# Two denoiser layers on one core: where the branch products of a weight piece stand in TensorE's order

## Chip, core and metric

The kernel runs on one core of a Trainium2 chip. The metric is the time of one execution on the device in microseconds. Three runs of the kernel before gave 1427.73, 1430.44 and 1431.5; the median is 1430.44.

## What is computed

Two layers run over 640 tokens: 128 of a context and 512 latent ones. Each layer normalises and modulates the tokens, projects them, runs four token mixers (A convolution, B grouped attention, C retention, D differential attention), projects each mixer's output to 1024 columns, weighs it with a sigmoid gate made from the same input, adds the four and projects the sum. What the change touches is this (cut from the reference):

```python
gates = jax.nn.sigmoid(h @ p["w_mgate"])
merged = None
for i, y in enumerate(branches):
    term = gates[..., i * D_MODEL:(i + 1) * D_MODEL] * (y @ p["w_branch"][i])
    merged = term if merged is None else merged + term
out = merged @ p["w_out"]
```

## The kernel before, in words

All activations lie in SBUF with tokens or features on the partitions. Every large product is made in about fp32 precision out of three products of a high and a low part: each weight piece of 256 columns is loaded raw, ScalarE makes its high part w_hi (L876) and VectorE its low part w_lo (L1086), piece by piece ("split").

The order of all work is one list, `plan`, built by `make_plan` and numbered by `number`. Each engine walks the same list and does its own share of every step, in the list's order, and waits by semaphores for what other engines do. So where a step stands in the list is where it stands in every engine's queue.

A weight piece with gates (function `gates`) holds 256 columns of `w_mgate` and the same 256 of `w_branch`. It is worked off in four **units** (two blocks of 128 columns by two halves of 320 tokens). The gate product of a unit has three **passes** of eight matmuls (L1437): pass 0 and pass 1 are the steps "pass", pass 2 is the step "gate". It alternates between the PSUM banks G0 and G1. ScalarE then takes the tanh (L963). The step "branch" has TensorE multiply the mixer's output y with `w_branch` (L1451, six matmuls into the bank BK); VectorE multiplies the result by the gate out of BK. For the first branch of a layer (A) that is one step (L1187), for the other three a step that frees BK (L1190) and an addition into `merged` (L1194). The product needs BK to have been read since the last one, and y's low part y_lo (L1216, step "ysplit").

`units` writes a piece as groups: pass 0, pass 1, then gate and branch together. In a layer there are four branches of four pieces, in the order A, D, B, C, so 64 products in a layer and 128 in all. Functions `spread` and `staged` put side work behind the groups: the attention of D beside branch A's pieces, the attention of B beside branch D's, and the retention of C beside branch B's. Branch C's pieces have none. Side work is made of the steps "cat" and "turn" (L973, L1250, L1493: rotate and transpose queries or keys), "map" (scores L1510 to L1513, their maximum L1258, their exp L999), "comb" (scale, L1267 or L1273), "pt" and "pv" (transpose L1519, value product L1532), and for retention "rscore" (L1571), "rout" (L1579, L1581, copied by L1358), "onorm" (L1306, with a power on POOL, L762) and "yturn".

The list further has steps that fall due after so many passes: the load of the next piece, its splits, and in some pieces the modulation of the next layer ("adav", VectorE's sums L1110; "adas", TensorE's transposes L1480 and their reduction L1116 and L1117). They stand right behind the pass that makes them due. At the end of a layer `merged` is split into h_hi and h_lo ("msplit", L1022 and L1362): tiles 0 and 1 after pass 0 and pass 1 of the last unit, the other three after its branch product. Then comes the output projection (L1435), whose results VectorE takes out (L1371).

Of the kernel before, what the change touches and what calls it, by code (L numbers as in the profile page):

```python
# [146 lines left out]
def make_plan():  # L147
# [3 lines left out]
    def chunk(l, src, col, branch=None):  # L151
        c = Step("load", l=l, n=n_chunk[0], src=src, col=col, branch=branch)
        n_chunk[0] += 1
        return c
# [7 lines left out]
    for l in range(DEPTH):  # L162
# [28 lines left out]
        for q in range(4):  # L191
            c = chunk(l, "w_out", q * CW)
            p9.append((c, [[Step("out", l=l, n=c.n, t=t, q=q)] for t in range(NT)]))

        def units(ch):

            out = []
            for c, us in ch:
                for k, u in enumerate(us):
                    out += [[("chunk", c, 2, 1)] * (k == 0) + [Step("pass", l=l, n=c.n, q=0, of=u[0])], [Step("pass", l=l, n=c.n, q=1, of=u[0])], u]  # L200
            return out

        def pair(two):

            (ck, _), (cq, _) = two
            k, q = units(two[:1]), units(two[1:])
            k[0][0], q[0] = ("chunk", ck, 1, 1), q[0][1:]
            q[9] = [("chunk", cq, 1, 1)] + q[9]
            kt, qt = ([sum(x[3 * t:3 * t + 3], []) for t in range(NT)] for x in (k, q))
            out = [kt[0]]  # L210
            for t in range(NT - 1):
                out += [kt[t + 1], qt[t]]
            return out + [qt[NT - 1]]

        body = []

        u = units(p1)
        flat = lambda groups: [s for g in groups for s in g]
        if l == 0:
# [15 lines left out]
        for i, unit in enumerate(pr):  # L235
# [4 lines left out]
            if l > 0 and i in (2, 4):  # L240
                t = 2 + i // 2
                body += [Step("xscale", l=l, t=t + 1)] * (t + 1 < NT) + [Step("hturn", l=l, t=t)]
        body += [Step("decays")] * (l == 0)
        u = units(pa)
        for t in range(1, NT):
            u[2 * t - 1] = u[2 * t - 1] + [Step("vec", l=l, br="D", t=t, part=1)]
# [28 lines left out]
        u = units(p6)  # L275
# [4 lines left out]
        u = units(p8)  # L280
# [8 lines left out]
        u = units(p9)  # L289
# [20 lines left out]
    out, due, passes = [], [], 0  # L310
    for e in plan:
        if isinstance(e, tuple):
            _, c, delay, gap = e

            if later and (c.branch in (1, 2) or (c.src == "w_in" and C_Q <= c.col < D_Q)):
                l, a, kh = later.pop(0)
# [1313 lines left out]
```

## Time and profile before

| | |
|---|---|
| median of three runs | 1430.44 us (1427.73 to 1431.5) |
| the profiled execution | 1431.54 us |
| its span, first to last instruction | 1429.3 us |
| TensorE busy | 1366.3 us, 96% |
| VectorE busy | 864.7 us, 60% |
| ScalarE busy | 570.4 us, 40% |
| POOL busy | 77.5 us, 5% |
| mean granted TensorE clock | 0.996 |

The profile is of one execution. Times in its rows are microseconds from the start of the span unless a row says ns. PE is TensorE, PEld its weight loads, DVE VectorE, ACT ScalarE, POOL GpSimd. Ends of matmuls are modelled, so neighbouring matmuls overlap in the rows; what counts for the pace is the distance between starts. The page has busy times, the chain of work that ended last, and groups of instructions. Beside the page there are views of the trace: waits by engine, the chain in order of time, and a timeline.

### The profile page before, as it was taken

What the parts mean: (1) busy time and instruction counts of PE and PEld (TensorE: products, weight loads), DVE (VectorE), ACT (ScalarE), POOL (GpSimd) and SP (SyncE); (2) the same over time, 40 slices, a digit from 0 to 9 for tenths busy, and PEclk for the clock granted to TensorE, in tenths of its full rate; (3) what the DMA queues carried; (4) which work ended last, traced back from release to release, by engine and by line L of the source; (5) the groups of instructions that cost most, each with busy time, mean ns of one, the idle gap of its engine ahead of it and who ended that gap; (6) DMA issues with size and microseconds to landing.
All of it is one profiled execution on the core that took longest, in us unless ns stands there. A gap on an engine that the chain in (4) does not pass through costs nothing.

```text
span 1429.3 us, 27105 instructions
## 1 busy us (share of the span) xinstructions
PE 1366.3 (96%) x10357; PEld 1320.5 (92%) x10357; DVE 864.7 (60%) x1764; ACT 570.4 (40%) x1252; POOL 77.5 (5%) x102
## 2 busy tenths in 40 slices
PE   5899999999999999999999999999999999999998
PEld 2799889999989999999999988999998999999998
DVE  2566676556555598777565467754755567654355
ACT  2566555334453222213343555542445422222242
POOL 0100000010000000100010000001100000001000
PEclk9999999999999999999999999999999999999999
DMA  9412212123012342465232211112221134213322
GB/s 320 151 59 64 75 38 67 33 72 111 30 30 93 126 137 70 130 175 176 71 119 79 88 43 57 55 60 74 75 67 31 34 120 143 75 50 106 121 72 75
DMA packets 106308, 127.71 MB, mean 89 GB/s; under 512 B 4076, under 2 KB 92744, under 8 KB 106184
## 3 DMA queue, kind: packets, MB, share of 16 engines
q1 hardware_dynamic: 101560, 110.76, 24.2%
q0 software_dynamic: 4624, 15.22, 3.6%
q8 instruction: 86, 1.41, 0.4%
q14 instruction: 38, 0.31, 0.1%
HBM read 119.66 MB, written 6.31 MB: 88 GB/s over the span
## 4 chain that ended last, share of the span: by engine, by line
PE 78%; DVE 11%; issue 5%; ACT 4%; POOL 1%; DMA 0%; DVEq 0%; SPq 0%; ACTq 0%; POOLq 0%
PE G L1437 37%; PE G L1435 19%; PE BK L1451 8%; PE TO L1532 3%; PE TP L1519 3%; PE TP L1493 2%; PE S L1510 1%; DVE w_lo L1086 1%; DVE neg_max L1258 1%; POOL rs L753 1%; PE BK L1462 1%; PE S L1513 1%; PE S L1512 1%; DVE h_lo L1362 1%; ACT w_hi L876 1%
## 5 line engine op out<-in xcount | busy, mean ns | idle before, releaser
L1086 DVE TENSOR_TENSOR w_lo<-w_raw,w_hi 128x512 fp32r<-128x512 f32 x312 | 208.2, 688 | 116.5 <-ACT w_hi L876 115.3
L1437 PE MATMUL G<-h_lo,w_hi 128*128 128x320 f32 x1472 | 248.9, 311 | 0.0
L1437 PE MATMUL G<-h_hi,w_lo 128*128 128x320 f32 x1472 | 248.7, 311 | 0.0
L1437 PE MATMUL G<-h_hi,w_hi 128*128 128x320 f32 x1472 | 248.1, 311 | 0.0
L1437 PEld LDWEIGHTS G<-h_lo,w_hi 128*128 128x128 f32 x1472 | 223.0, 188 | 0.5
L1437 PEld LDWEIGHTS G<-h_hi,w_lo 128*128 128x128 f32 x1472 | 223.1, 188 | 0.2
L1437 PEld LDWEIGHTS G<-h_hi,w_hi 128*128 128x128 f32 x1472 | 222.0, 188 | 0.8 <-issue 0.3
L876 ACT ACTIVATE w_hi<-w_raw 128x512 fp32r<-128x512 f32 x312 | 184.9, 623 | 18.9 <-DMA w_raw<-in_w_branch 13.7
L963 ACT ACTIVATE tg<-G 128x320 f32<-128x320 f32 x128 | 55.7, 435 | 237.4 <-PE G L1437 236.0
L1435 PE MATMUL G<-w_hi,h_hi 128*128 128x256 f32 x960 | 138.3, 287 | 5.0 <-DVE ra L1371 3.2
L999 ACT ACTIVATE work<-S,neg_max 128x640 f32<-128x640 f32 (+1 forms) x120 | 85.1, 710 | 144.2 <-DVE neg_max L1258 129.8
L1435 PE MATMUL G<-w_hi,h_lo 128*128 128x256 f32 x960 | 136.1, 285 | 0.1
L1435 PE MATMUL G<-w_lo,h_hi 128*128 128x256 f32 x960 | 135.1, 283 | 0.0
L1435 PEld LDWEIGHTS G<-w_hi,h_hi 128*128 128x128 f32 x960 | 125.0, 194 | 6.8 <-DVE ra L1371 3.9
L1435 PEld LDWEIGHTS G<-w_hi,h_lo 128*128 128x128 f32 x960 | 124.4, 193 | 0.7 <-DVE h_lo L1171 0.7
L1435 PEld LDWEIGHTS G<-w_lo,h_hi 128*128 128x128 f32 x960 | 123.7, 192 | 0.0
L1190 DVE SCALAR_TENSOR_TENSOR tg<-tg,BK 128x320 f32<-128x320 f32 x96 | 46.7, 487 | 104.3 <-PE BK L1451 94.9
L1258 DVE TENSOR_REDUCE neg_max<-S 128x1 f32<-128x640 f32 x96 | 78.7, 819 | 25.2 <-PE S L1513 23.2
L1110 DVE SCALAR_TENSOR_TENSOR ada_sum<-w_raw,cond_w,ada_sum 128x512 f32<-128x512 f32 x112 | 78.9, 746 | 1.9
L1006 ACT ACTIVATE work<-TP 128x640 f32<-128x640 f32 (+1 forms) x80 | 49.6, 620 | 61.0 <-PE TP L1519 60.6
L1451 PE MATMUL BK<-y_hi,w_hi 128*128 128x320 f32 x256 | 58.6, 310 | 4.6 <-DVE y_lo L1216 4.6
L1519 PE MATMUL TP<-cst,work 128*128 128x128 f32 x336 | 51.5, 278 | 9.3 <-ACT q_stack L983 8.3
(226 smaller groups left out, 1589.9 us busy)
## 6 DMA issues: line engine op xcount, KB each, us to landing
w_raw<-in_w_mgate SPq DMA_DIRECT2D x32, 1024.0 KB, 5.4
w_raw<-in_w_in SPq DMA_DIRECT2D x30, 1024.0 KB, 5.5
w_raw<-in_w_ada SPq DMA_DIRECT2D x17, 1024.0 KB, 5.3
w_raw<-in_w_branch SPq DMA_DIRECT2D x32, 256.0 KB, 5.8
w_raw<-in_w_out SPq DMA_DIRECT2D x8, 1024.0 KB, 4.9
early_raw<-in_w_ada SPq DMA_DIRECT2D x6, 1024.0 KB, 11.8
work<-in_x_sample POOLq DMA_DIRECT2D x4, 512.0 KB, 6.0
work<-gate_rows POOLq DMA_DIRECT2D x4, 512.0 KB, 5.0
```

What stands on the lines that cost most here:

```text
L876: nc.scalar.activation(w_hi[:, s.n % 2, a:b, :], raw_rows(s), ACT.Copy).then_inc(hi_done, 1)
L963: nc.scalar.activation(tg[:, s.tg % 2, :], g[:, 0:HALF], ACT.Tanh, scale=0.5).then_inc(big_evac, 1)
L999: nc.scalar.activation(dst, src, ACT.Exp, bias=neg_max[:, col:col + 1], accum_out=e_sum[:, col:col + 1]).then_inc(exp_done, 1)
L1006: nc.scalar.activation(p_slot(s.head)[:, 0:n], TP[:, 0:n], ACT.Copy).then_inc(tp_evac, 1)
L1086: V.tensor_tensor(w_lo[:, s.n % 2, a:b, :], raw_rows(s), w_hi[:, s.n % 2, a:b, :].bitcast(F32), ALU.subtract).then_inc(lo_done, 1)
L1110: V.scalar_tensor_tensor(out=ada_sum[:, c, :], in0=row, scalar=w, in1=ada_sum[:, c, :], op0=ALU.mult, op1=ALU.add).then_inc(ada_added, 1)
L1190: V.scalar_tensor_tensor(out=t_, in0=t_, scalar=1.0, in1=BK[:, 0:HALF], op0=ALU.add, op1=ALU.mult).then_inc(bk_evac, 1)
L1258: V.tensor_reduce(neg_max[:, col:col + 1], S[:, :].rearrange("p (a n) -> p a n", a=2)[:, :, 0:HALF], AX.XY, ALU.max, negate=True).then_inc ...
L1435: ins = mm(g[:, 0:CW], a[:, kt, t], b[:, w, kt, :], start=first, stop=last)
L1437: ins = mm(g[:, 0:HALF], a[:, w, kt, c], b[:, kt, half], start=first, stop=last)
L1451: ins = mm(BK[:, 0:HALF], a[:, w, KT + kt, c], b[:, kt, half], start=i == 0 and kt == 0, stop=i == 2 and kt == 1)
L1519: ins = nc.tensor.transpose(TP[:, i * P:(i + 1) * P], e_slot(s.es)[:, i * P:(i + 1) * P], ident)
```

## The change

Within a weight piece the branch product of units 0, 1 and 2 no longer stands right behind the unit's gate product, but behind the first pass of the next unit. Unit 3 of a piece keeps gate and branch together. Side work that `spread` puts behind the gate's group now comes ahead of that pass and of the product. Steps due at the pass (splits, modulation, loads) come ahead of the product too. Pieces without gates are as they were, since their units have one step.

```diff
             out = []
             for c, us in ch:
+                held = []
                 for k, u in enumerate(us):
-                    out += [[("chunk", c, 2, 1)] * (k == 0) + [Step("pass", l=l, n=c.n, q=0, of=u[0])], [Step("pass", l=l, n=c.n, q=1, of=u[0])], u]
+                    out += [[("chunk", c, 2, 1)] * (k == 0) + [Step("pass", l=l, n=c.n, q=0, of=u[0])] + held, [Step("pass", l=l, n=c.n, q=1, of=u[0])]]
+                    held = u[1:] if k + 1 < len(us) else []
+                    out += [u[:1] if held else u]
             return out
```

## Rows read from the trace of the kernel before

**Rows 1.** The page's first part: busy us, share of the span, instructions.

```profile
PE 1366.3 (96%) x10357; PEld 1320.5 (92%) x10357; DVE 864.7 (60%) x1764; ACT 570.4 (40%) x1252; POOL 77.5 (5%) x102
```

**Rows 2.** Chain of waits in order of time, in branch C: start, us, what.

```profile
613.00 3.52 PE G L1437 x24
617.40 3.52 PE G L1437 x24
```

**Rows 3.** Waits of TensorE: who, for what, us in total, times, longest.

```profile
PE BK L1451 <- DVE y_lo L1216: 4.6, 4, 1.6
```

**Rows 4.** Timeline, branch C's first unit: start, us, what [idle before, releaser]; layers 0, 1.

```profile
603.98 1.42 PE L1437 MATMUL G<-h_hi,w_lo 128*128 128x320 f32 x8
607.04 0.53 PE L1451 MATMUL BK<-y_hi,w_hi 128*128 128x320 f32 x2 [1.65 <-DVE y_lo L1216]
...
1296.23 0.54 PE L1451 MATMUL BK<-y_hi,w_hi 128*128 128x320 f32 x2 [0.63 <-DVE y_lo L1216]
```

**Rows 5.** Timeline, branch A's first unit, layer 0.

```profile
206.09 0.42 DVE L1250 TENSOR_TENSOR work<-za,work 128x256 fp32r<-128x256 f32 x1
...
207.27 0.60 PE L1493 MATMUL TP<-cst,work 128*128 128x128 f32 x4
```

**Rows 6.** Timeline, branch A's first piece, units 1 to 3, layer 0.

```profile
215.93 0.49 DVE L1187 SCALAR_TENSOR_TENSOR merged<-tg,BK 128x320 f32<-128x320 f32 x1
...
216.37 0.69 DVE L1086 TENSOR_TENSOR w_lo<-w_raw,w_hi 128x512 fp32r<-128x512 f32 x1
...
217.96 0.82 DVE L1258 TENSOR_REDUCE neg_max<-S 128x1 f32<-128x640 f32 x1
...
219.51 0.19 ACT L999 ACTIVATION_READ_ACCUMULATOR work<-S,neg_max 128x1 f32 x1
...
220.06 0.54 PE L1510 MATMUL S<-k_stack,q_stack 128*128 128x320 f32 x2
```

**Rows 7.** Timeline, branch D's second piece, behind unit 2, layer 0.

```profile
373.33 0.19 ACT L999 ACTIVATION_READ_ACCUMULATOR work<-S,neg_max 128x1 f32 x1
...
373.66 0.39 PE L1512 MATMUL S<-k_stack,q_stack 128*128 128x320 f32 x1
```

**Rows 8.** Timeline, branch D's third piece, unit 3's first pass and behind it, layer 0.

```profile
407.23 1.33 PE L1437 MATMUL G<-h_hi,w_hi 128*128 128x320 f32 x8
...
408.36 0.55 DVE L1267 TENSOR_SCALAR work<-work,e_inv 128x640 f32<-128x640 f32 x1
...
409.06 0.74 PE L1519 MATMUL TP<-cst,work 128*128 128x128 f32 x5 [0.49 <-DVE work L1267]
```

**Rows 9.** Timeline, branch B's third piece, unit 1, layer 0.

```profile
560.46 0.69 DVE L1116 TENSOR_REDUCE mod<-S 128x4 f32<-128x512 f32 x1 [0.60 <-PE S L1480]
...
561.60 0.72 PE L1571 MATMUL S<-work 64*128 64x128 f32 x8 [0.96 <-DVE mod L1117]
```

**Rows 10.** Timeline, branch B's last piece, units 2 and 3, layer 0.

```profile
596.81 0.42 DVE L1358 COPY o_s<-TO 128x256 f32<-128x256 f32 x1 [0.46 <-PE TO L1581]
...
599.88 2.93 DVE L1110 SCALAR_TENSOR_TENSOR ada_sum<-w_raw,cond_w,ada_sum 128x512 f32<-128x512 f32 x4
...
600.18 0.46 PE L1451 MATMUL BK<-y_hi,w_hi 128*128 128x320 f32 x2
```

**Rows 11.** Timeline, end of layer 1.

```profile
1358.98 0.49 DVE L1190 SCALAR_TENSOR_TENSOR tg<-tg,BK 128x320 f32<-128x320 f32 x1 [2.79 <-PE BK L1451]
...
1363.40 0.48 DVE L1190 SCALAR_TENSOR_TENSOR tg<-tg,BK 128x320 f32<-128x320 f32 x1
...
1370.02 1.22 PE L1435 MATMUL G<-w_hi,h_hi 128*128 128x256 f32 x8 [0.93 <-DVE ra L1371]
```

**Rows 12.** Timeline, end of layer 0.

```profile
676.96 0.48 DVE L1190 SCALAR_TENSOR_TENSOR tg<-tg,BK 128x320 f32<-128x320 f32 x1
...
684.37 1.86 PE L1435 MATMUL G<-w_hi,h_hi 128*128 128x256 f32 x7 [2.30 <-DVE ra L1371]
```

## Prediction

> **What bounds the kernel now.** The page's busy shares come first: TensorE is busy for 96% of the span, VectorE for 60% and ScalarE for 40% [rows 1]. The chain of waits then gives the pace where nothing disturbs it: 24 matmuls of one gate unit take 3.52 us, and the next unit starts 4.40 us after this one [rows 2]. So one matmul costs 3.52 / 24 = 0.147 us, one pass of eight 1.17 us, and the six of a branch product 4.40 - 3.52 = 0.88 us. That 0.88 holds two changes of PSUM bank and two waits, so a change of bank costs nothing that can be seen. The list of TensorE's waits is read last, since only its idle time can be won or lost. The branch product itself waited four times, 4.6 us in all, always for y_lo [rows 3]. I measure waits below by the issue pace (start of the last pass plus 1.17). Ends of matmuls are modelled, so this gives somewhat more than the idle time printed.
>
> **What the change does to the queues.** It adds and removes no instruction. In each weight piece the products of units 0, 1 and 2 move behind the next unit's first pass (96 of 128 products, 1.17 us later). Side work that stood between the product and that pass moves 0.88 us ahead. VectorE's two steps on a product (L1190 and L1194, 0.49 us each) move behind whatever is due at that pass: weight splits (L1086, 0.69 us each), the modulation sums (L1110, 1.4 us for two), and the side work's maxima and copies. ScalarE has no step for a product. No DMA moves, and SP and POOL hold no step that waits for a product of units 0 to 2. Where no side work stands, TensorE's total is the same and I cost the move at nothing; the cover is that one product's bank is read out long before the next. Between units 2 and 3 that cover shrinks from 3.52 to 2.35 us (two passes), of which VectorE's read-out takes an estimated 0.7 (its 0.49 and the signal).
>
> **Waits for y_lo.** The unit-0 product of branch C stands right behind its gate unit. In layer 0 the last pass starts at 603.98 and so ends at 605.15; the product starts at 607.04: 1.89 waited, where 1.65 is printed [rows 4]. The pass covers 1.17, and TensorE comes to this place 0.70 late (below): -1.87. In layer 1 the product starts at 1296.23 after 0.63 printed, an estimated 0.8 by issue, covered whole by the pass: -0.80.
> Branch A's unit-0 product is different. Side work follows it: a transpose of catb, at 207.27, that waits for VectorE's lower part, which runs 206.09 to 206.51, behind y_lo [rows 5]. With the product gone from before it, this transpose waits until about 206.65, so it and what follows start only 0.62 sooner, while the product's 0.88 comes later on top. The wait is not saved but handed on: **+0.26** in each layer.
>
> **A score product too early.** In branch A's first piece the scores of 220.06 need an exp that ended at 219.70 [rows 6]. Without the 0.88 of unit 2's product they would start at 219.18, so even with VectorE unchanged they wait about 0.6. VectorE changes too: now it does the product's step at 215.93 while ScalarE is still making w_hi, then w_lo at 216.37, and the maximum at 217.96. After the change w_lo comes first and can't start before 216.37, so the step of 0.49 falls behind it, and the maximum and the exp move by about 0.6 plus the 0.26 above. I get the scores at 220.6, and 220.6 - 219.18 - 0.26 = **+1.16** in each layer. Bounds: 0.6 (the step hides) and 1.6 (another 0.49 on the chain).
> Together for branch A: 2 x (0.26 + 1.16) = +2.84.
>
> **Branch D.** The scores at 373.66 start as their exp ends at 373.52 [rows 7]; the product before them covers nothing that they need later, so taking it away leaves them where they are and the product's 0.88 comes on top: +0.88. One wait goes: the transpose of 409.06 waited for VectorE's scaling of 408.36 to 408.91 [rows 8]; it stands behind the pass, where the product now comes between. The pass started at 407.23, so the wait by issue is 409.06 - 408.40 = 0.66, less than 0.88: -0.66. Sum 0.22 a layer, +0.44. The waits behind an evacuated q_stack stay, as transpose and evacuation stay neighbours.
>
> **Branch B, layer 0.** The retention scores at 561.60 waited 0.96 for the modulation sum that VectorE began at 560.46 [rows 9]. The transposes which feed it now run 0.88 before, with the product behind them: -0.94. Against that, in its last piece VectorE copies the retention output at 596.81, has the normaliser's round trip to POOL and then the modulation sums from 599.88 [rows 10]. The copy and all behind it come 0.88 sooner, so the sums start at 599.00 and two of the four take 1.4, and only then comes unit 2's step: about 600.33 to 600.81. Unit 3's product, which started at 600.18, needs it: **+0.70**. Layer 1 has no such sums there.
> The Trainium skill bears on this (TensorE: Matmul & The Clock Gate, section "Architectural detail: the array is 16x 32x32, not 1x 128x128"): ScalarE's and VectorE's queues are strictly first in, first out. By it, a step held for its product also holds all that is behind it. If VectorE could step past, the 0.70 would be gone and the sum 1.9; the order of the steps in the trace agrees with the rule.
>
> **The end of a layer.** The first two splits of the merged tensor wait for unit 14's product, whose VectorE step started at 1358.98; behind them stands unit 15's, at 1363.40, and at the end of that chain the third token tile of the output projection, at 1370.02 after 0.93 idle [rows 11]. Unit 14's product comes 1.17 later, and nothing in the chain between has room: +1.17. In layer 0 unit 15's step started at 676.96, late because VectorE had modulation sums in between, and the tile waited 2.30 [rows 12]; VectorE now idles for 1.1 before the first split and does the same work: +1.10. Together +2.27.
>
> **Sum.** -0.80 - 1.87 + 2.84 + 0.44 - 0.94 + 0.70 + 2.27 = +2.6 us. The profiled execution took 1431.54 (span 1429.3 and 2.2 around it), so it would be 1434.1; it stands 1.1 above the median of 1430.44, and from that I forecast 1433.0.
>
> **Rivals.**
> (1) *Hidden anyway.* The queues re-form: a step that waits at one place finds room at the next, and the early side work gives back what its waits cost. For: 96% busy, and most side steps have 1 to 3 us of room. Against: the losses above are idle time of TensorE itself. Time: +-1 around 1430.4. Chance 0.22.
> (2) *The gains stay, the losses don't.* The maxima and exps all run sooner than I think, and ScalarE splits in time. Then -0.80 - 1.87 - 0.94 - 2 x 0.66 = -4.9, with the end of the layer (the surest loss) still +2.27: -2.7, 1427.7; without that too 1425.5. Chance 0.08.
> (3) *Slower by a closed bank.* The product of unit 3 waits for VectorE's read of unit 2's. Its room falls from 3.52 - 0.69 = 2.83 to 1.66 us, and it decides wherever VectorE is later than that. In layer 0 of branches B and C eight pieces put 1.4 us of sums ahead of that step; if not one but all pay 0.70, the sum grows by 7 x 0.70 = 4.9 to +7.5: 1437.9. For it: VectorE is late in both places shown [rows 10, 12]. Against: in the other seven the sums run while TensorE is in the pass, as they wait for no product. Chance 0.15.
> (4) *It doesn't do what it says*: the products stay, or the order of a pair is bound by another wait. The plan is a list, walked by every engine, so this has 0.01, at 1430.4.
> The forecast, +1 to +5.5, has 0.54.
>
> **How the numbers follow.** A measurement of this kernel tells about 0.3% (4.3 us) from no change. Faster by more needs rival 2 in full: 0.04. Slower by more is rival 3 and the upper quarter of the forecast: 0.15 + 0.14 = 0.29. The rest, 0.67, is within. The range leaves out the full rival 2 and the far end of rival 3: 1428.5 to 1437.5.
>
> **What would show it.** The list of waits loses "BK L1451 <- y_lo" in whole (4.6 us). In branch A's first piece a catb transpose waits about 1.5 and a score product about 1.2. In branch D the scores near 374 wait about 0.8 and the transpose near 409 no more. The third tile of the output projection waits 3.4 and 2.1 instead of 2.30 and 0.93. TensorE's busy time stays at 1366. The prediction is wrong if unit 3's products wait in many pieces (rival 3), if the pace of 4.40 a unit in branch C changes, or if the end of the layer is not later.

## The result, and the profile after

| | before | changed |
|---|---|---|
| median | 1430.03 us, 16 runs (1427.73 to 1431.55) | 1433.15 us, 16 runs (1430.91 to 1433.92) |
| profiled execution | 1431.54, span 1429.3 | 1433.37, span 1430.9 |
| mean granted clock | 0.996 | 0.998 |

The ratio is 1.0019 [1.0011, 1.0027]. The changed kernel is slower by 3.1 us, which is a real difference and lies within 0.3%. The forecast was 1433.0. One execution of the kernel before, in a later series, took 2677.85 us and one of the variant without the last product 3396.68 us; the ratios leave these two out.

The page's first part, of the changed kernel (before: [rows 1]):

```profile
PE 1367.3 (96%) x10357; PEld 1320.6 (92%) x10357; DVE 866.3 (61%) x1764; ACT 570.4 (40%) x1252; POOL 77.5 (5%) x102
```

The same instructions and the same work. TensorE's waits, of the changed kernel (for what, us in total, times, longest):

```profile
PE S L1513 <- ACT work L1002: 9.2, 14, 1.1
...
PE TP L1496 <- DVE work L1253: 8.1, 12, 2.1
...
PE G L1438 <- DVE ra L1374: 5.5, 2, 3.4
...
PE BK L1454 <- DVE tg L1193: 0.5, 1, 0.5
```

Lines below the diff stand 3 higher than before: L1454 is the branch product of L1451. The wait of the product for y_lo [rows 3] is no longer in the list. In its place stand longer waits for the output projection, for a transpose and for scores, and one wait of 0.5 us for VectorE's read of the bank BK.

The places that were foretold, in the changed kernel's timeline (start, us, what, [idle before, releaser]). First branch A, for [rows 5] and [rows 6]:

```profile
206.81 0.42 DVE L1253 TENSOR_TENSOR work<-za,work 128x256 fp32r<-128x256 f32 x1
...
207.38 0.63 PE L1496 MATMUL TP<-cst,work 128*128 128x128 f32 x4 [1.49 <-DVE work L1253]
...
217.10 0.69 DVE L1089 TENSOR_TENSOR w_lo<-w_raw,w_hi 128x512 fp32r<-128x512 f32 x1 [0.56 <-ACT w_hi L879]
...
217.70 0.48 DVE L1190 SCALAR_TENSOR_TENSOR merged<-tg,BK 128x320 f32<-128x320 f32 x1
...
219.09 0.82 DVE L1261 TENSOR_REDUCE neg_max<-S 128x1 f32<-128x640 f32 x1
...
220.63 0.19 ACT L1002 ACTIVATION_READ_ACCUMULATOR work<-S,neg_max 128x1 f32 x1
...
220.88 0.56 PE L1513 MATMUL S<-k_stack,q_stack 128*128 128x320 f32 x2 [0.44 <-ACT work L1002]
```

The transpose now waits 1.49 (foretold: about 1.5). VectorE splits first and takes the product's result second, as foretold, but the scores wait only 0.44. Branch D, behind unit 2 of its second piece, for [rows 7]:

```profile
373.46 1.33 PE L1440 MATMUL G<-h_hi,w_lo 128*128 128x320 f32 x8
...
374.59 0.29 DVE L1270 TENSOR_SCALAR work<-work,e_inv 128x128 f32<-128x128 f32 x1
375.03 0.30 PE L1522 MATMUL TP<-cst,work 128*128 128x128 f32 x1 [0.23 <-DVE work L1270]
375.22 0.19 ACT L1002 ACTIVATION_READ_ACCUMULATOR work<-S,neg_max 128x1 f32 x1
...
375.46 0.42 PE L1515 MATMUL S<-k_stack,q_stack 128*128 128x320 f32 x1
```

The pass before them started at 373.46, so by the pace it ended at 374.63. TensorE then waited for a scaled row (375.03), did that one transpose and began the scores at 375.46, as their exp ended at 375.41.

Branch B's last piece, for [rows 10], and the third output tile at the end of each layer, for [rows 11] and [rows 12]:

```profile
600.16 1.41 DVE L1113 SCALAR_TENSOR_TENSOR ada_sum<-w_raw,cond_w,ada_sum 128x512 f32<-128x512 f32 x2
...
601.49 0.48 DVE L1193 SCALAR_TENSOR_TENSOR tg<-tg,BK 128x320 f32<-128x320 f32 x1
...
602.02 0.56 PE L1454 MATMUL BK<-y_hi,w_hi 128*128 128x320 f32 x2 [0.52 <-DVE tg L1193]
...
685.50 1.22 PE L1438 MATMUL G<-w_hi,h_hi 128*128 128x256 f32 x8 [3.36 <-DVE ra L1374]
...
1371.61 1.22 PE L1438 MATMUL G<-w_hi,h_hi 128*128 128x256 f32 x8 [2.10 <-DVE ra L1374]
```

The sums at 600.16 stand ahead of the read-out at 601.49, and unit 3's product stands behind both.

**The account by steps.** Laid side by side matmul by matmul, the two traces keep a constant distance in time except at a few places. The jump of that distance at a place is its price, called a step from here on (taken at starts, so a little other than the idle time printed):

| place | foretold | changed kernel |
|---|---|---|
| A, transpose, each layer | +0.26 | +0.29 |
| A, scores, each layer | +1.16 | +0.71 |
| D, scores near 374, each layer | +0.88 | +0.83, and +0.12 at a transpose shortly ahead |
| D, transpose near 409, each layer | -0.66 | -0.68 |
| B, retention scores, layer 0 | -0.94 | -0.88 |
| B, unit 3's product, layer 0 | +0.70 | +0.79 |
| C, y_lo, layers 0 and 1 | -1.87, -0.80 | -1.89, -0.87 |
| end of layers 0 and 1 (from the waits) | +1.10, +1.17 | +1.06, +1.17 |
| sum | +2.6 | +1.9 |

Everywhere else, at most of the 96 moves, the distance stays the same. The steps give 1.9, the medians 3.1. What makes the other 1.2 is asked below.

### The profile page after: what moved, and what is told of

Same layout as the page of the kernel before. It is cut to its first block, busy times and chain, and to the rows that moved or that the text cites. A ratio compares the mean times of both kernels' runs of the same rounds, so it can differ in the third digit from the quotient of the medians.

```text
span 1430.9 us, 27105 instructions
## 1 busy us (share of the span) xinstructions
PE 1367.3 (96%) x10357; PEld 1320.6 (92%) x10357; DVE 866.3 (61%) x1764; ACT 570.4 (40%) x1252; POOL 77.5 (5%) x102
## 3 DMA queue, kind: packets, MB, share of 16 engines
q8 instruction: 86, 1.41, 0.4%
## 4 chain that ended last, share of the span: by engine, by line
PE 79%; DVE 10%; issue 5%; ACT 4%; POOL 1%; DMA 0%; DVEq 0%; SPq 0%; ACTq 0%; POOLq 0%
PE G L1440 37%; PE G L1438 19%; PE BK L1454 8%; PE TO L1535 3%; PE TP L1522 3%; PE TP L1496 2%; PE S L1513 1%; DVE w_lo L1089 1%; DVE neg_max L1261 1%; POOL rs L756 1%; PE BK L1465 1%; PE S L1515 1%; ACT work L1002 1%; ACT w_hi L879 1%; PE S L1516 1%
## 5 line engine op out<-in xcount | busy, mean ns | idle before, releaser
L1089 DVE TENSOR_TENSOR w_lo<-w_raw,w_hi 128x512 fp32r<-128x512 f32 x312 | 211.4, 689 | 156.2 <-ACT w_hi L879 154.7
L1454 PE MATMUL BK<-y_hi,w_hi 128*128 128x320 f32 x256 | 58.9, 311 | 0.5 <-DVE tg L1193 0.5
```

The source lines that it names most:

```text
L1089: V.tensor_tensor(w_lo[:, s.n % 2, a:b, :], raw_rows(s), w_hi[:, s.n % 2, a:b, :].bitcast(F32), ALU.subtract).then_inc(lo_done, 1)
L1454: ins = mm(BK[:, 0:HALF], a[:, w, KT + kt, c], b[:, kt, half], start=i == 0 and kt == 0, stop=i == 2 and kt == 1)
```

## The experiments

The line that decides which products are held is, in the changed kernel, `held = u[1:] if k + 1 < len(us) else []`. Most edits add a condition to it; every engine still walks the one list, but for the two kernels where this is said.

**The changed kernel again.**

> The changed kernel once more, to tell its fixed part from what one execution adds. Theory (a sum of single waits): every step between the two traces repeats to 0.1 us: branch A +1.0 a layer, branch D +0.3 a layer, branch B and C in layer 0 -0.9, +0.8 and -1.8, branch C in layer 1 -0.9, the ends of the layers +1.1 and +1.2; together +2.0, and the median 2 to 3 us above the kernel before. Rival (the difference is chance of the clock at the start and at the end of layer 0): the steps move about by more than 0.3, and the medians differ by under 1 us.

Measured: 1433.11 against 1429.92, ratio 1.0023 [1.0015, 1.0032]. Its steps are those of the table within 0.02, up to the end of layer 0. There the two executions of one program part. TensorE's busy time and granted clock (PEclk, behind the bracket) at the end of layer 1, first the changed kernel's own profile, then this one:

```profile
1370.00:1376.00 6.00, 4.34 (x34) 1.00 0.25 87
```

```profile
1370.00:1376.00 6.00, 5.06 (x30) 0.72 0.28 87
```

Behind the same wait of 2.10 the clock stays at 2.4 GHz in one and falls to 1.2 GHz for a while in the other, and the tile's first eight matmuls take 1.78 us where they took 1.22:

```profile
1370.94 1.78 PE L1438 MATMUL G<-w_hi,h_hi 128*128 128x256 f32 x8 [2.10 <-DVE ra L1374]
```

The end of layer 1 so costs 2.34 instead of 1.17. This term was missing from my sum. The runs with unit 14 at the end of this section ask for it.

**One branch at a time.** The conditions were `and c.branch == 0` (A), `== 3` (D), `== 1` (B) and `== 2` (C).

> The change in branch A's pieces alone. Theory: +0.3 (the wait for y_lo handed to the transpose behind it) and +0.7 (scores that come before their exp) in each layer, +2.0 in the steps of the trace; waits of 1.5 at the transpose and 0.4 at the scores. Rival (these losses come from the queues being shifted in all branches): under +0.5 here.

> The change in branch D's pieces alone. Theory: +0.1 (a transpose of queries), +0.8 (scores that start as their exp ends) and -0.7 (a transpose that waited for a scaled row) in each layer, +0.3 a layer. Rival (interaction with branch A before it): other steps, or none.

> The change in branch B's pieces alone. Theory: in layer 0 -0.9 at the third retention score and +0.8 at unit 3's product of the last piece, which waits about 0.5 for VectorE's step on unit 2's; as TensorE is then 0.8 late at branch C's first product, the wait there for y_lo (1.65 printed) shrinks to about 0.9; nothing in layer 1. Rival: the product doesn't wait, the step of +0.8 belongs to branch C.

> The change in branch C's pieces alone. Theory: -1.5 to -1.8 in layer 0 and -0.9 in layer 1 at the first product, +1.1 at the end of layer 0 and +1.2 at the end of layer 1; in sum about 0. Rival (the end of a layer is late because of what came before): -2.5 with waits at the ends of 2.3 and 0.9 as in the kernel before.

Measured, one execution each: 1431.19, 1429.47, 1429.48 and 1431.41, beside 1429.37 for the kernel before; single times scatter by more than these terms, so the steps are read. A alone: +0.29, +0.70 in layer 0 and +0.28, +0.71 in layer 1. D alone: +0.12, +0.84, -0.68 in each. B alone: -0.88, +0.79, and -0.94 at C's y_lo, because a late TensorE finds less to wait for. Those of A and D and the first two of B are the steps of the full change. C alone gives -1.60 instead of -1.89 in layer 0 and then something that the full change has not, a wait for the bank BK in C's first piece. It costs 0.84, and 0.13 more a little later. The timeline of the kernel with C alone:

```profile
616.52 1.41 DVE L1113 SCALAR_TENSOR_TENSOR ada_sum<-w_raw,cond_w,ada_sum 128x512 f32<-128x512 f32 x2
...
617.85 0.48 DVE L1193 SCALAR_TENSOR_TENSOR tg<-tg,BK 128x320 f32<-128x320 f32 x1
...
618.38 0.56 PE L1454 MATMUL BK<-y_hi,w_hi 128*128 128x320 f32 x2 [0.58 <-DVE tg L1193]
```

VectorE's read-out of unit 2's product (617.85) stands behind the modulation sums, and unit 3's product (618.38) waits for it. This is rival 3's closed bank, with 0.58 of wait. In the full change TensorE comes 0.79 later, from B's last piece, and finds the bank free. With this, and with a fall of the clock behind the wait of 2.10 at the end of layer 1, C alone comes to +1.7 in its trace, where about 0 was expected.

**Without the last product.** The condition was `and (c.branch, c.col % DM // CW, k) != (2, 3, 2)`: only unit 14, the third unit of C's last piece, goes back to its old place.

> The change, but unit 2 of branch C's last piece keeps its product behind its gate unit, so that the first splits of the merged tensor start as before. Theory: the third token tile of the output projection waits 2.3 and 0.9 us again instead of 3.4 and 2.1, all else as changed: 2.3 us below the changed kernel, 0.3 below the kernel before, which can't be told from it. Rival (the layer's end is late for another reason, such as the delays before it): those waits stay at 3.4 and 2.1 and the time equals that of the changed kernel.

Measured: 1429.70, ratio 0.9998 [0.9989, 1.0007]. All other steps are as in the changed kernel, and the tile's waits are back:

```profile
1368.11 1.10 PE L1438 MATMUL G<-w_hi,h_hi 128*128 128x256 f32 x7 [0.93 <-DVE ra L1374]
```

By the steps this should win 1.06 + 1.17 = 2.2 against the changed kernel; it wins 3.4 (1433.11 and 1429.70 on the same chip). By its steps it should stand 0.3 below the kernel before, and it stands 0.2 below. So in this kernel steps and medians agree, as they do in the next one, and in the changed kernel they don't.

**Chosen moves.** `and (c.branch, c.col % DM // CW, k) in ((2, 0, 0), (1, 2, 0), (3, 2, 2))`: only the three products (in each layer) whose move the trace shows as a gain.

> Only four places of each layer's 48 products, those where a wait was gained, keep the new position (branch C's first unit, unit 0 of branch B's third piece, unit 2 of branch D's third piece: three kinds, six places in both layers, of which five count). Theory: -1.5 and -0.9 for y_lo, -0.9 for the modulation sum, -0.7 twice for the scaled row, nothing lost: -4.7 us, ratio 0.9967. Rival (what is gained at one place is waited for at the next, since the queues behind it are in step): under 1.5 us gained, and new waits of 0.3 or more behind the four places.

Measured: 1425.39, ratio 0.9968 [0.9956, 0.998]. The steps are -0.68, -0.88, -1.59, -0.68, -0.87, in sum -4.7, and no new wait. It is 4.5 us faster than the kernel before and 7.7 than the changed one, on the same chip. The span is 1422.8, with

```profile
PE 1364.4 (96%) x10357; PEld 1320.1 (93%) x10357; DVE 864.7 (61%) x1764; ACT 570.7 (40%) x1252; POOL 77.7 (5%) x102
```

**One pass further.** The held product stands behind pass 1 instead of pass 0, but for unit 14:

```diff
-... [Step("pass", l=l, n=c.n, q=0, of=u[0])] + held, [Step("pass", l=l, n=c.n, q=1, of=u[0])]]
+... [Step("pass", l=l, n=c.n, q=0, of=u[0])] + held * end, [Step("pass", l=l, n=c.n, q=1, of=u[0])] + held * (not end)]
```

> The products of units 0 to 2 behind the next unit's second pass instead of its first (the last one of branch C stays behind the first). Between unit 2's and unit 3's product stands one pass, 1.17 us. Theory of the bank's room (2.83 us before, 1.66 changed, about 0.5 here): unit 3's product now waits wherever VectorE is over half a microsecond late, above all in the pieces of layer 0 with modulation sums (2.8 us of them stand ahead of VectorE's step): six or more waits of 0.3 to 1.5 us there, 3 to 8 us in all on top of the changed kernel. Rival (the bank never matters, only the order of side work does): no product waits, and the time is within 1.5 us of the changed kernel's.

Measured: 1441.69, ratio 1.0083 [1.0069, 1.0096]. That is 8.6 over the changed kernel, where 3 to 8 was expected, but with two waits for the bank instead of six or more. The bank closes in B's second and last piece of layer 0, with 1.90 and 2.05 of wait. Timeline of the first, and then TensorE's windows around it (us, busy, PEclk, DMA):

```profile
550.23 1.41 DVE L1114 SCALAR_TENSOR_TENSOR ada_sum<-w_raw,cond_w,ada_sum 128x512 f32<-128x512 f32 x2
551.55 0.48 DVE L1194 SCALAR_TENSOR_TENSOR tg<-tg,BK 128x320 f32<-128x320 f32 x1
...
552.09 0.73 PE L1455 MATMUL BK<-y_hi,w_hi 128*128 128x320 f32 x2 [1.90 <-DVE tg L1194]
```

```profile
550.00:552.00 2.00, 0.19 (x2) 1.00 0.96 331
552.00:554.00 2.00, 1.91 (x8) 0.58 0.53 96
554.00:556.00 2.00, 2.00 (x11) 0.57 1.03 400
556.00:558.00 2.00, 2.00 (x20) 1.00 0.11 38
```

The place costs 3.7 us: the 1.90 of the wait, and 1.8 behind it, where the granted clock is 0.58 over four microseconds (an estimated 4 x 0.42 = 1.7 of work lost). The second costs 3.9, with the clock at half speed behind it too. Rival 3's mechanism is real; with one more pass it opens in two pieces, not in all eight.

**VectorE's order alone, TensorE's order alone.** In the first, the kernel before with VectorE walking a list whose branch steps stand behind the next unit's first pass and what is due at it; in the second, the changed kernel with VectorE's branch steps right behind the gate step, as before.

```diff
-            for s in plan:
+            for s in branch_later(plan):
```

```diff
-            for s in plan:
+            for s in branch_first(plan):
```

> TensorE's order as before; only VectorE's steps on the products of units 0 to 2 move to where the change puts them, behind the next unit's first pass and what falls due at it. No product moves, no matmul waits for another reason. It measures VectorE's part by itself. Theory: at branch A's scores (0.25 us of room) a wait of 0.2 to 0.3 in each layer; unit 3's product of branch B's last piece in layer 0 waits about 1.5, since the read of unit 2's stands behind 1.4 us of sums; the end of layer 0 about +1, the end of layer 1 nothing; +2 in all, with none of the gains (y_lo still waits at two of four places). Rival (VectorE's order is free, only TensorE's matters): no step over 0.1.

> TensorE's order as changed, VectorE's as before: VectorE's step on a product stands first in its queue, and the product comes about 2 us later, behind side work and a pass. Theory (VectorE takes its queue strictly in order): the maxima, copies and splits behind it are held until the product is done, the scores that follow wait up to 1 us at some five places in each of branches A and D of a layer, and the time is 4 to 15 us over the changed kernel. Rival (steps that are ready pass the one that waits): the waits are those of the changed kernel without the one at unit 3's product in branch B, and the time is at or 1 us below it.

Measured: 1435.37, ratio 1.004 [1.0025, 1.0055], and 1468.7, ratio 1.028 [1.0262, 1.0298]. The sizes expected of both were too small. VectorE's order alone costs 5.7 us, not 2: +0.25 at branch A's scores and +0.29 at a product of its next piece, in each layer, and two longer waits for the bank, 1.21 in B's second piece and 1.41 in its last (+1.47 and +1.68), since here the products stand ahead of the pass and VectorE's read-outs behind it. The end of layer 0, expected at +1, did not move (a wait of 2.33 against 2.30), and C's wait for y_lo in layer 0 shrank (-0.92). All its steps sum to 4.0. The span of its profile is 4.9 longer than that of the kernel before: 4.0 from the steps and 0.9 from start-up, which differs from one execution to the next. How much of the other 1.7 in the medians is start-up stays open. TensorE's order alone costs 35.6 us over the changed kernel, not 4 to 15. VectorE holds at its branch step until the product comes, a pass and its side work later, and the splits, maxima and scalings stand behind it. Waits of that kernel:

```profile
PE TP L1533 <- DVE work L1281: 19.8, 16, 2.8
PE S L1524 <- ACT work L1013: 10.8, 16, 1.1
PE TP L1507 <- DVE work L1264: 9.3, 14, 2.1
```

The transposes behind VectorE's scaling (L1281) waited 16 times, 19.8 us; in the changed kernel twice, 0.5. That is the strict order of VectorE's queue (the Trainium skill, TensorE: Matmul & The Clock Gate, section "Architectural detail: the array is 16x 32x32, not 1x 128x128") with its price: a step held for its product does hold all that is behind it.

**Unit 14 alone.** The converse of *Without the last product*: `and (c.branch, c.col % DM // CW, k) == (2, 3, 2)`, and the same in layer 1 only, `and (l, c.branch, c.col % DM // CW, k) == (1, 2, 3, 2)`.

> Only one of the 96 moves of the change is made, in each layer: the product of the third unit of branch C's last piece (unit 14) stands behind the first pass of unit 15. Nothing is left out of the computation. Theory of the layer's end with its clock: the third tile of the output projection waits 3.4 and 2.1 instead of 2.30 and 0.93 (+1.06 and +1.17 against the kernel before), and behind the wait of 2.1 in layer 1 the granted clock falls to 0.5 once, in four of five such profiles so far and in none of seven with 0.93, for about 1.2 us more. So the time is +2.2 from the steps and +0.9 from the clock on the mean, +3.1 in all, about 1433.0 beside a kernel before of 1430.0, ratio 1.0022. Rival, the clock's fall comes by chance and is the same for both kernels: +2.2, ratio 1.0015, and the profile shows no fall near 1371. Rival, the loss at the end is made elsewhere and only shows there: ratio 1.0000.

> The same single move as in the run beside it, but in layer 1 alone; layer 0 is as in the kernel before. Nothing is left out of the computation. Theory: the third tile waits 2.30 in layer 0 and 2.1 in layer 1, +1.17 from the step, and +0.9 on the mean (1.2 where it happens) from a granted clock that falls to 0.5 behind the wait near 1371: +2.1, ratio 1.0015. Rival, no more falls than in the kernel before: +1.17, ratio 1.0008, granted clock 1.0 from 1366 to 1374.

Measured: 1434.63, ratio 1.0029 [1.0015, 1.0043], and 1431.16, ratio 1.0007 [0.9998, 1.0016]. One move of 96, made in both layers, costs 4.1 us (interval 2.1 to 6.2), no less than the whole change (1.6 to 3.9). The profile of the first has both ends late and both at the lower clock:

```profile
684.00:687.00 3.00, 3.00 (x15) 3.00 (x16) 2.63 (x7) 1.55 (x4) 0.00 (x0) 0.50 0.00 0
...
1370.00:1374.00 4.00, 2.57 (x13) 2.57 (x14) 2.87 (x6) 1.55 (x4) 0.53 (x1) 0.72 0.34 131
```

(here with all engines' busy times; PEclk is the third number from the right). By steps it is +2.03 in layer 0, of which 1.06 is the wait, and +2.34 in layer 1, of which 1.17 is: 4.4. In layer 1 alone the wait is 2.09, the step is +1.17, and the clock does not fall:

```profile
1370.00:1374.00 4.00, 3.95 (x33) 3.75 (x32) 2.05 (x4) 2.37 (x7) 0.00 (x0) 1.00 0.34 131
```

So the rival of no more falls held in that kernel's profile, and its median (+0.65, interval -0.3 to +2.3) fits it, though the +2.1 of the theory lies inside the interval too. The fall of the clock is a matter of odds, not a fixed price: of the six times of the kernel with both moves, five lie between 1433.85 and 1436.23 and one at 1430.63; that one's mean granted clock is 0.991, where the profiled execution has 0.987.

## Why the prediction was right, and where it was not

**What bounds the kernel.** Right. The pace of 4.40 us a unit in branch C is unchanged. The chain of the changed kernel there, in order of time:

```profile
613.35 0.88 PE BK L1454 x6
614.23 3.52 PE G L1440 x24
617.75 0.88 PE BK L1454 x6
618.63 2.35 PE G L1440 x16
```

3.52 and 0.88 as before [rows 2]. The move itself, with its changes of bank at another place, costs nothing.

**The waits for y_lo.** Right: gone in branch C (-1.89 and -0.87), handed on in branch A (+0.29 net of a new wait of 1.49).

**Branch A's scores.** The term was mis-sized: +1.16 foretold, +0.71 measured. The step that failed is "the maximum and the exp move by about 0.6 plus the 0.26 above". Clear of 0.73 that this profile is later from its start-up, the scores start at 220.88 - 0.73 = 220.15, not 220.6. The same working then gives 220.15 - 219.18 - 0.26 = 0.71. Two parts of it were too large. The 0.26 belongs to TensorE alone: the split of the weight ran at 217.10 - 0.73 = 216.37, the very time of before [rows 6], as ScalarE and VectorE were not held up with it. And the product's step, moved behind the split, delayed the maximum by 219.09 - 0.73 - 217.96 = 0.40, not 0.6. VectorE's order alone costs 0.25 here, so the larger part is TensorE's early arrival.

**Branch D.** Right within 0.1: +0.83 and -0.68. It came out 0.12 a layer worse, since a transpose behind an evacuated q_stack waits 0.79 where it had waited 0.69; I had said that these waits stay.

**Branch B.** Right in both: -0.88 and +0.79. The wait for the bank is there as foretold, once, in the last piece of layer 0.

**The end of a layer.** The waits were right: 3.36 and 2.10 for a foretold 3.4 and 2.1. Unit 14 alone produces them, unit 14 left in place takes them away. Their price was not right. I counted TensorE's idle time only and not the clock behind it. The tile's wait of 2.10 in layer 1 stands in seven profiles with unit 14 moved; behind it the clock fell in five (all but the changed kernel's own and the one of layer 1 alone). The wait of 0.93 stands in seven others, and it fell in none. One fall cost 1.17 there (2.34 against 1.17 in two executions of one program). In layer 0 the clock had fallen behind the wait of 2.30 already in the kernel before, in its profile and in five of seven others; with 3.4 it fell in five of six, and in two of these for twice as long, for another 0.97.
The odds then give, for layer 1, 5/7 x 1.17 = 0.8, and for layer 0 (3 x 1.16 + 2 x 2.13) / 6 - 6/8 x 1.16 = 0.4, with 1.16 for one fall (worked out under *The sum*) and 1.16 + 0.97 = 2.13 for the long one. That is 1.2 in all: 1.9 + 1.2 = 3.1, as measured. The counts are small, so the split between the layers is an estimate. Against it stands the kernel with unit 14 alone, whose 4.1 is near both falls in full.

The mean granted clock of the executions without a trace points the same way. Start-up splits them into two groups: the traces with a mean below 0.992 have a stretch at the lower clock on record from about 24 to 44 us, the others have none. In the lower group the kernel before has 0.989 or 0.990 in all of its 33 executions of the later series. The changed kernel has 0.987 in 8 of 17, and these take 1433.19 to 1433.94, while its other nine take 1430.91 to 1432.89. So in the same program a lower clock goes with the longer time. That the two falls account for all of the 1.2 is an estimate.

**The sum.** Branch A was foretold 0.8 too high, the others together 0.1 too low, and the clock was missing with about 1.2. The errors cancel in part: the medians differ by 3.1, where 2.6 was foretold. That the median itself was hit to 0.2 us is luck twice over, since the base of the forecast, 1430.44 from three runs, lay 0.4 above the 1430.03 of sixteen. In the profiled executions they show apart. The changed one's span is 1.6 longer: 0.73 from the start-up, 1.9 from the steps, less 1.16 for the fall at 684 that the kernel before had and it had not (across that tile the distance between the traces went down by 0.10, where the longer wait alone would have added 1.06).

**The rivals.** *Hidden anyway* fell: the losses stayed, and the steps added up. The queues do act on each other in two places, which the runs by branch show: B's delay takes 0.94 off C's wait for y_lo in layer 0, and it keeps the bank free in C's first piece. *The gains stay, the losses don't* fell as a forecast; as a choice it is true, by leaving the losing moves out. *The closed bank* was right as a mechanism and wrong in its reach. It bites once in the change, once more in a piece of C where C moves alone, and twice, for 3.7 and 3.9 us, one pass further. What protects the other pieces is, I think, what I gave: their sums run while TensorE is in the pass. No run tried that by itself.

## What to carry to other kernels

Where one engine is busy for 96%, a rule that moves a step everywhere is worth only what it does at the few places where that engine waits: eight kinds of place decided here, and three moves in each layer picked from the trace give -4.5 us where all 96 give +3.1. The step on which an end of a layer hangs must not be moved back even by one pass, and a side step must not be moved ahead of the thing it waits for. And a wait at TensorE is to be priced with the clock behind it, which at the end of layer 1, where it fell, added as much again (1.17) as the wait had grown.

## What the runs showed of the hardware

The granted clock falls from 2.4 to 1.2 GHz behind single waits in the midst of a kernel that is 96% busy: behind 1.90 and 2.05 in branch B of the kernel with one pass further, behind 2.10 at the end of layer 1 in five of seven profiles, not behind 1.65 (the kernel before, at 607). A wait of 2.10 near 96 us stands in all fourteen profiles, those of the kernel before and the changed one among them, and the clock fell behind it in seven. Behind the waits of 1.3 to 1.7 us that these profiles have after 60 us it fell in none. The length of a wait alone does not decide it. In the kernel with TensorE's order alone the same transpose waits 2.79 in both layers of one execution. Its windows behind the wait, layer 0 and then layer 1:

```profile
416.00:418.00 2.00, 1.30 (x10) 1.00 0.00 0
418.00:420.00 2.00, 2.00 (x16) 1.00 0.03 8
...
1128.00:1130.00 2.00, 1.69 (x10) 0.71 0.00 0
1130.00:1132.00 2.00, 2.00 (x9) 0.50 0.00 0
```

In layer 0 the clock stays and eight matmuls a microsecond run; in layer 1 it falls and nine take two. By the account of steps this place costs 2.29 in layer 0 and 3.83 in layer 1, so the fall costs 1.54 here. The Trainium skill (TensorE: Matmul & The Clock Gate, section "What's actually happening") says that the gate counts activity in a time of its own, which does not restart with the kernel. The runs agree with that: the same wait, in two executions or twice in one, comes out with a fall and without. What phase decides was not tried.
